# Chained matrix products on one Trainium2 core: when the squares, the mean, the root and the input splits are issued

## What is computed

```python
def rmsnorm(x, g):
    xf = x.astype(F32)
    y = xf * lax.rsqrt(jnp.mean(xf * xf, axis=-1, keepdims=True) + NORM_EPS)
    return (y * g.astype(F32)).astype(x.dtype)

def conv_glu(hn, w_in, conv_w, conv_b, w_out):
    u, gate_in = jnp.split(hn @ w_in, 2, axis=-1)
    c = (conv_w[0] * shift_right(gate_in, 2) + conv_w[1] * shift_right(gate_in, 1)
         + conv_w[2] * gate_in + conv_b)
    return (jax.nn.gelu(c, approximate=False) * u) @ w_out
...
        h = h + mix
        h = h + conv_glu(rmsnorm(h, ffn_norm[i]), ffn_w_in[i], ffn_conv_w[i], ffn_conv_b[i], ffn_w_out[i])
        e = rmsnorm(p[i] @ ple_w_proj[i], ple_norm[i])
        gate = jax.nn.sigmoid(rmsnorm(h, ple_gate_norm[i]) @ ple_w_gate[i])
        h = h + gate * e
```

## Time and profile before

| | |
|---|---|
| median of 3 runs | 2211.72 us |
| profiled execution, its own time | 2205.65 us |
| its span | 2203.5 us |
| PE busy | 2002.1 us, 91% of the span |
| PEld busy | 1915.2 us, 87% |
| DVE busy | 1479.8 us, 67% |
| ACT busy | 1208.4 us, 55% |
| granted PE clock, mean | 0.954 of full |

### The profile page before, as it was taken

One profiled execution on the slowest core, in us unless ns is written; L12 is line 12 of the kernel. 1 busy time (PEld: TensorE's weight loads), 2 busy tenths in 40 slices (PEclk: granted clock), 3 DMA queues, 4 the chain that ended last, 5 costly groups with the idle time before them and its releaser, 6 DMA issues. The chain is left out here.

```text
span 2203.5 us, 43929 instructions
## 1 busy us (share of the span) xinstructions
PE 2002.1 (91%) x15940; PEld 1915.2 (87%) x15940; DVE 1479.8 (67%) x3041; ACT 1208.4 (55%) x2342; POOL 0.2 (0%) x4
## 2 busy tenths in 40 slices
PE   6998888999999898999999896897998988899896
PEld 6887778999999867999999796897998977799896
DVE  4667655999755598666666577754687667468865
ACT  4455544777765597555555456102555544655654
POOL 0000000000000000000000000000000000000000
PEclk9999999999999999999999997976999999799998
DMA  5433434455566400656555361001565633146562
GB/s 179 145 101 106 123 107 125 153 181 171 181 191 192 151 0 30 188 184 188 183 187 184 114 192 48 1 1 39 165 194 155 194 102 107 37 159 195 162 189 66
DMA packets 96222, 295.97 MB, mean 134 GB/s; under 512 B 9315, under 2 KB 25830, under 8 KB 95974
## 3 DMA queue, kind: packets, MB, share of 16 engines
q1 hardware_dynamic: 96102, 294.35, 42.9%
HBM read 293.26 MB, written 1.05 MB: 134 GB/s over the span
## 5 line engine op out<-in xcount | busy, mean ns | idle before, releaser
L449 PE MATMUL bank<-a_high,w_high 128*128 128x256 f32 x3256 | 933.8, 287 | 108.2 <-DVE w_low L423 65.8
L423 DVE TENSOR_TENSOR w_low<-ring,w_high 128x512 fp32r<-128x512 f32 x1102 | 746.9, 689 | 423.0 <-ACT w_high L417 417.3
L450 PE MATMUL bank<-a_low,w_high 128*128 128x256 f32 x3256 | 915.2, 281 | 0.0
L451 PE MATMUL bank<-a_high,w_low 128*128 128x256 f32 x3256 | 914.7, 281 | 0.0
L417 ACT ACTIVATE w_high<-ring 128x512 fp32r<-128x512 f32 x1102 | 676.5, 627 | 433.8 <-PE bank L451 430.1
L449 PEld LDWEIGHTS bank<-a_high,w_high 128*128 128x128 f32 x3256 | 625.7, 192 | 128.6 <-DVE w_low L423 73.0
L450 PEld LDWEIGHTS bank<-a_low,w_high 128*128 128x128 f32 x3256 | 624.5, 192 | 0.6
L451 PEld LDWEIGHTS bank<-a_high,w_low 128*128 128x128 f32 x3256 | 624.1, 192 | 0.0
L449 PE MATMUL bank<-s_high,w_high 128*128 128x256 f32 x1024 | 287.8, 281 | 2.0 <-DVE s_low L2195 2.0
L450 PE MATMUL bank<-s_low,w_high 128*128 128x256 f32 x1024 | 287.7, 281 | 0.0
L451 PE MATMUL bank<-s_high,w_low 128*128 128x256 f32 x1024 | 287.7, 281 | 0.0
(11 more groups left out here) (350 smaller groups left out, 2036.5 us busy)
## 6 DMA issues: line engine op xcount, KB each, us to landing
ring<-in_stream SPq DMA_DIRECT2D x279, 512.0 KB, 3.6
ring<-in_peer_u SPq DMA_DIRECT2D x128, 512.0 KB, 3.5
ring<-in_peer_v SPq DMA_DIRECT2D x128, 512.0 KB, 3.5
ring<-in_stream SPq DMA_DIRECT2D x32, 256.0 KB, 3.2
x<-in_x SPq DMA_DIRECT2D x4, 256.0 KB, 5.7
arena<-in_mem SPq DMA_DIRECT2D x1, 1024.0 KB, 11.7
out<-x SPq DMA_DIRECT2D x4, 256.0 KB, 2.6
consts<-in_consts SPq DMA_DIRECT2D x1, 640.0 KB, 8.5
```

The source lines that it names most:

```text
L423: self.nc.vector.tensor_tensor(self.w_low[:, h % SLOTS, :], self.raw(h), self.w_high[:, h % SLOTS, :].bitcast(F32), ALU.subtract)\
L449: self.nc.tensor.matmul(to, lh, rh, start=start, stop=False, **more)
L450: self.nc.tensor.matmul(to, lh, rl, start=False, stop=False, **more)
L451: return self.nc.tensor.matmul(to, ll, rh, start=False, stop=stop, **more)
```

## The change

Four things change in how the duties are made; the instructions of PE, and the order of PE, are the same as before.

- An input chunk that has a key is split right after the duty that makes it, and no longer at the earliest 3 halves before its product starts. Inputs without keys of the same segment come no later than the first of them.
- The squares of a norm are made in parts of two chunks, one part behind each of four successive halves. The norm of `e` in PLE, the double norm of the hybrid mixer and the two norms of the MLA products keep one square.
- The mean (DVE) comes one half later, and the root (ACT) two halves later. For the double norm and the MLA norms both stay.
- "root" on DVE is now the duty "mean".

```diff
+        early = min([s[0].keys[0] for s in sources if isinstance(s[0], (Normed, Later)) and s[0].keys]
+                    + [N_GROUPS * 2])
         for source, at, chunks, start, _, slot in sources:
             first_key = start - AHEAD if before is not None else max(start - AHEAD, s0)
             keys = source.keys if isinstance(source, (Normed, Held, Later)) else ()
             for c in range(chunks):
-                key = first_key + c // HALF, 0
-                if keys:
-                    key = max(key, (keys[c], 5))
+                key = (keys[c], 5) if keys else (min(first_key + c // HALF, early), 0)
                 duties.append(key + ("input", (source, c, slot + c)))
         for i, (_, start, u) in enumerate(norms):
-            known = (max(start, norms[i][0].keys[-1]), 5) if norms[i][0].keys else (start, 2)
-            duties += [known + ("squares", i), (units[u].end + 1, 2, "root", i)]
+            norm = norms[i][0]
+            wide = isinstance(norm, Twice) or norm is also or brief
+            known = (norm.keys[-1], 5) if norm.keys else (start, 2)
+            for c in range(0, norm.chunks, norm.chunks if wide else 2):
+                key = known if wide else max(known, (start + 1 + c // 2, 2))
+                duties.append(key + ("squares", (i, c, norm.chunks if wide else c + 2)))
+            late = 0 if wide and norm is not also else 1
+            duties += [(units[u].end + 1 + late, 2, "mean", i), (units[u].end + 1 + 2 * late, 2, "root", i)]
...
-                nc.scalar.activation(squared[what][:, 0:norm.chunks, :],
-                                     norm.source[:, 0:norm.chunks, :], ACT.Square)\
-                    .then_inc(squares.up(), 1)
+                ins = nc.scalar.activation(squared[i][:, c0:c1, :], norm.source[:, c0:c1, :],
+                                           ACT.Square)
+                if c1 == norm.chunks:
+                    ins.then_inc(squares.up(), 1)
...
-            elif kind == "root":
+            elif kind == "mean":
                 dve.wait_ge(sums.sem, sums.at(what + 1))
```

More of the change, by code:

```diff
@@ L867, in on_act @@
             elif kind == "squares":
-                norm = norms[what][0]
-                if what and norm is not also and not brief:
-                    act.wait_ge(sums.sem, sums.at(what))
+                i, c0, c1 = what
+                norm = norms[i][0]
+                if i and norm is not also and not brief:
+                    act.wait_ge(sums.sem, sums.at(i))
                 if norm is also:
@@ L873, in on_act @@
                         act.wait_ge(copied[e].sem, copied[e].at(copies(1, 1, e)))
-                for sem, value in norm.ready[-1:]:
+                for sem, value in norm.ready[c1 - 1:c1]:
                     act.wait_ge(sem, value)
```

## The result

The changed kernel took 2188.3 us (median of 4 executions), the kernel before 2209.7 in the same comparison: ratio 0.9903, interval 0.9875 to 0.9930. The forecast was 2202.5, with a range of 2190 to 2212: the time lies 1.7 us under the range and 14.2 us under the forecast, on the side of a larger gain. The profiled execution took 2192.9 us, 12.7 less than that of before, where the sum said 9.2.

A forecast was written before the change was run, and what follows sets the result against it. PE was taken as the bound, losing time where weight splits come late. The terms summed to -9.2 us: 2196.5 from the profiled 2205.65, and 2202.5 us for a median, with a range of 2190 to 2212.

The forecast's parts named there:

- squares, three passages: Two passages to `ffn_in` and one to `mem_q`: squares in four parts let PE's half come 1.80 us earlier, -5.4 us.
- `peer_q`, end of `mem_q`, PLE: Later mean and root save PE's waits: -1.5 us in `peer_q`, -1.1 in `mem_q`, -3.2 in PLE's two layers; together -5.8.
- first mixer: Later roots and squares in parts together bring the first mixer's late half 3.3 us earlier, with more after: -5.7 us.
- pairs behind additions to x: In `ffn_out`, `hyb_out`, `mla_o` and `w_out`, input splits made behind an addition to x delay the next half: +6.3 us.
- units of `ffn_in`, first unit included: Input splits behind a unit's last product lengthen each unit by 0.82 us, +12.9; the first units' earlier chain gives -0.5.
- ends of `ffn_in`: Input splits no longer bunch at the end of `ffn_in`; its 16 halves take 25.3 us: -10.4 us over both layers.
- small places: The pair in `w_out` behind the branches costs 0.9 us; PLE squares and MLA norms' later inputs save 1.5: -0.6.
- the unit as a chain of 11.7: A unit of `ffn_in` is bound by a chain of waits of 11.7 us, where PE needs 10.88.
- Rival A: Units of `ffn_in` don't get longer because ACT and DVE close up: -22 us, 2190 us; chance 0.17.
- Rival B: The clock falls once in each unit of `ffn_in` because of its stall: +16 us, 2219 us; chance 0.12.
- Rival C: The end of `ffn_in` gains only half, about 7 of 10.4 us lost: -2 us, 2210 us; chance 0.11.
- the upper case that the prediction named: At the end of `ffn_in` the clock falls again in one layer: +1.7 us.

The follow-up runs named there:

- q_after: The changed kernel plus an unused reciprocal stalling PE 0.32 us in each round of the loop from 870 to 1240 us: 2203.9 us, ratio to before 0.9988.
- q_before: The kernel before plus an unused reciprocal stalling PE 0.32 us in each round of the loop from 870 to 1240 us: 2222.3 us, ratio 1.0059.
- c_after: The changed kernel, unchanged, profiled a second time: 2189.6 us, ratio to the kernel before 0.9881.
- e1: The kernel before with only the input splits moved to where their chunk is made: 2216.0 us, ratio 1.0034.
- e4: The kernel before with only the mean one half and the root two halves later: 2185.2 us, ratio 0.9895.
- e2: The changed kernel with the input splits as they were before: 2176.1 us, ratio to the kernel before 0.9848; run again, 2182.6 us, ratio 0.9901.

## Why the prediction was wrong

By its own steps, with the mean of four traces with the change (q_after among them) less the mean of three of before (q_before among them):

| term | forecast | traces |
|---|---|---|
| squares, three passages | -5.4 | -5.4 |
| `peer_q`, end of `mem_q`, PLE | -5.8 | -6.7 |
| first mixer | -5.7 | -4.8 |
| pairs behind additions to x | +6.3 | +5.8 |
| units of `ffn_in`, first unit included | +12.4 | +11.4 |
| ends of `ffn_in` | -10.4 | -9.5 |
| small places | -0.6 | about -0.6 |
| sum | -9.2 | -9.8 |

Each step holds, and the largest, the unit as a chain of 11.7, to 0.03 us. (Slips of the sum are tenths: 2 x 8 x 0.82 is 13.1, and 25.3 against 29.78 is -4.5. Windows over the same 16 halves give the ends -10.0 in the mean of these traces, since terms can be parted a few halves earlier or later.) Rival A named nearly the right time, 2190, for a reason that the trace refutes: its units did not keep their length. Of the 11.4 only 9.3 stand in the traces as stalls. The other 2.1 are matmuls at a longer distance, which at the short pace would be stall; the chain sets the unit's time at either pace. Rival B fell: the clock was 1.00 in all units ahead of the ends, in all four traces. Rival C fell with the ends at 25.5 and 25.3 us; the second end of c_after, with a fall of the clock in it, took 27.0, the upper case that the prediction named.

The step that failed is the one from the sum to a median: "The median of the runs shown is 6.1 above it, 2211.7, so the forecast for a median is **2202.5 us**." It took three executions for the kernel's level. They lay at 2211.7 in the median, while 89 have a mean of 2207.0 and a standard deviation of 7.9, and the 4 of after lay 3.5 under their kernel's 2191.8. That is 8.2 of the 14.2 us, and it is chance of the draw. The other 6.0 are the change itself: -15.2 (3.9) against -9.2. There a term failed that the sum put at nothing: the clock outside the end of `ffn_in`. The sum had 1.7 us of clock, all of it there; in the traces it is 5.9, of which 1.2 stand in the table's ends. With the other 4.7, and 1.0 us of small stalls the other way, -9.8 becomes -13.5, inside the interval of the executions. (The experiments' table has -16.0 for the same traces mainly because the 2.1 us of the units are pace there and left out.)

How much of the clock's part is the change's work differs from place to place. At the two passages to `ffn_in` the fall goes with the stall of 1.9 us: the five traces that have the stall (three of before, e1, e4) show a fall in 4 of 10 passages, the ten that don't have it in none of 20. At the ends of `ffn_in` it doesn't go with the change. The fall at 1695 in the earlier trace rows stands in all three traces of before and in none of the four with the change at that place, but one stands in the other layer's end in c_after, one in each of e1's two ends, where the input splits are moved too, and none in e4's, where they aren't. So the 1.7 us that the prediction gave the change there may be chance. The second end of c_after, then the ends of e4:

```profile
2071.68:2098.64 26.96, 24.46 (x193) 23.96 (x193) 19.88 (x36) 13.79 (x27) 0.00 (x0) 0.94 0.54 160
```
```profile
1665.23:1695.14 29.91, 23.89 (x194) 22.59 (x193) 25.28 (x53) 19.21 (x44) 0.00 (x0) 1.00 0.41 143
2057.27:2087.18 29.91, 23.84 (x195) 22.55 (x193) 25.29 (x53) 19.21 (x44) 0.00 (x0) 1.00 0.41 143
```

Windows of the second passage to `ffn_in`, before (its second trace) and then after:

```profile
1938.71:1953.22 14.51, 12.60 (x94) 12.39 (x93) 6.76 (x12) 7.01 (x11) 0.00 (x0) 0.88 0.56 178
```
```profile
1932.19:1943.17 10.98, 10.88 (x95) 10.66 (x93) 6.95 (x12) 7.07 (x14) 0.00 (x0) 1.00 0.72 211
```

Of these 3.5 us 1.8 are the stall and 1.6 the half clock behind it. What of the rest of the clock's part is the change's work, and what is chance, stays open: e2's executions show no higher mean clock, the changed kernel's 33 with q_after do. The prediction let rival B hold by the Trainium skill (TensorE: Matmul & The Clock Gate, section "A second HAM failure mode: psum-queue depth-cycling"), which tells of a kernel in which short idles between groups of matmuls came often enough to make the clock swing. Here 0.2 to 0.6 us of idle in each unit of 11.7 us left it at 1.00, so idles of this size and this frequency don't bear rival B out.

## What to carry to other kernels

Where several instructions wait for one another across two engines, put new work where one of them waits anyway, not behind the link that is made last: the same input splits cost 0.85 us a unit directly behind the product and nothing in the unit four halves later. Before a forecast is put on a level, ask how far single executions of the kernel before lie apart; three of them can miss it by half of what is to be predicted. A stall that brings a fall of the clock with it costs about twice what it shows, but the stall of 1.9 us here brought one in only 4 of 10 places.

## What the hardware showed

With nothing changed in its instructions, a stretch in which PE never waits ran at 1.360 or 1.413 us per 12 matmuls, at full clock: 13.6 us over the second loop. The pace stays while PE doesn't wait (362 us in one trace of before) and can change at a stall. What sets it was not found.
